# First groups of three weight units, square sums by matmul, and a boundary without GpSimd in a two-layer decoder step

## The reference, cut to what matters

```python
def rms_norm(x, g):
    return x * lax.rsqrt(jnp.mean(x * x, axis=-1, keepdims=True) + EPS) * g

for l in range(2):
    h = rms_norm(x, norm_mix_pre[l])
    mix = mixer_ab(h, ...) if l == 0 else mixer_c(h, ...)      # h @ w_in, mixing, @ w_out
    x = x + rms_norm(mix, norm_mix_post[l])
    h = rms_norm(x, norm_ffn_pre[l])
    a, b = jnp.split(h @ w_up, 2, axis=-1)
    a, new_prev = causal_dwconv(a, prev, conv_w)               # three taps along the tokens
    x = x + rms_norm((jax.nn.gelu(a) * b) @ w_down, norm_ffn_post[l])
```

## Time and profile before

| | us |
|---|---|
| median of 3 runs | 1489.02 (1487.93 to 1490.28) |
| the profiled execution | 1488.02 |
| its span, first to last instruction | 1486.2 |
| TensorE busy | 1394.4 (94% of the span) |
| VectorE busy | 867.9 (58%) |
| ScalarE busy | 557.0 (37%) |
| GpSimd busy | 318.5 (21%) |
| mean granted TensorE clock | 0.966 of 2.4 GHz |

### The profile page before, as it was taken

The page is one execution under the profiler, slowest core; times in us unless marked ns, Lnnn a source line. Parts: engine busy times, 40 slices in busy tenths (PEclk is TensorE's granted clock), DMA queues, the critical chain, the costliest instruction groups (busy, mean ns, idle before and its releaser), DMA issues.

```text
span 1486.2 us, 27553 instructions
## 1 busy us (share of the span) xinstructions
PE 1394.4 (94%) x10588; PEld 1357.5 (91%) x10588; DVE 867.9 (58%) x1319; ACT 557.0 (37%) x1022; POOL 318.5 (21%) x405
## 2 busy tenths in 40 slices
PE   9899997999999999977999999989799999999995
PEld 8887896999999999967899898889699999999995
DVE  6356538665656522268877878864766566563224
ACT  5234334433333322235544444433443333332221
POOL 2123224111111100143222223221511111111002
PEclk9989998999999999989999999989899999999998
DMA  7311131222222322221222212112122222233211
GB/s 262 102 34 53 58 88 37 90 85 87 92 88 85 117 94 82 75 72 57 73 86 86 83 68 78 60 72 87 44 84 87 92 90 85 85 111 110 78 39 60
DMA packets 38526, 123.32 MB, mean 83 GB/s; under 512 B 4104, under 2 KB 9864, under 8 KB 38344
## 3 DMA queue, kind: packets, MB, share of 16 engines
q1 hardware_dynamic: 31888, 110.74, 23.0%
q10 hardware_dynamic: 6408, 11.38, 2.1%
q0 software_dynamic: 176, 0.44, 0.1%
HBM read 113.98 MB, written 8.57 MB: 82 GB/s over the span
## 4 chain that ended last, share of the span: by engine, by line
PE 76%; DVE 15%; issue 4%; ACT 3%; ACTq 1%; DMA 0%; DVEq 0%; POOL 0%; SPq 0%
PE acc L365 67%; DVE w_lo L1036 2%; PE aux L576 2%; DVE x L1237 2%; DVE mix L1232 1%; DVE lev L1334 1%; PE aux L613 1%; PE acc L383 1%; DVE v_s L1489 1%; DVE scratch L1440 1%; DVE h_lo L1044 1%; DVE lev L1328 1%; PE aux L487 1%; DVE c_E L1491 1%; PE aux L467 1%
## 5 line engine op out<-in xcount | busy, mean ns | idle before, releaser
L1036 DVE TENSOR_TENSOR w_lo<-raw,w_hi 128x512 fp32r<-128x512 f32 (+1 forms) x372 | 320.5, 864 | 401.3 <-ACT w_hi L693 400.4
L365 PE MATMUL acc<-h_hi,w_hi 128*128 128x272 f32 x2208 | 477.1, 298 | 35.8 <-DVE h_lo L1044 32.2
L365 PE MATMUL acc<-h_hi,w_lo 128*128 128x272 f32 x2208 | 464.8, 293 | 0.0
L365 PE MATMUL acc<-h_lo,w_hi 128*128 128x272 f32 x2208 | 463.9, 292 | 0.0
L365 PEld LDWEIGHTS acc<-h_hi,w_hi 128*128 128x128 f32 x2208 | 355.4, 193 | 46.8 <-issue 26.5
L693 ACT CAST w_hi<-raw 128x512 fp32r<-128x512 f32 (+1 forms) x372 | 238.4, 643 | 423.4 <-PE acc L365 410.1
L365 PEld LDWEIGHTS acc<-h_lo,w_hi 128*128 128x128 f32 x2208 | 355.9, 193 | 0.0
L365 PEld LDWEIGHTS acc<-h_hi,w_lo 128*128 128x128 f32 x2208 | 353.1, 193 | 0.0
L365 PE MATMUL acc<-g_hi,w_lo 128*128 128x272 f32 x684 | 141.6, 288 | 0.0
L365 PE MATMUL acc<-g_hi,w_hi 128*128 128x272 f32 x684 | 141.4, 288 | 0.0
L365 PE MATMUL acc<-g_lo,w_hi 128*128 128x272 f32 x684 | 141.0, 288 | 0.0
(11 more groups left out here) (244 smaller groups left out, 1640.8 us busy)
## 6 DMA issues: line engine op xcount, KB each, us to landing
raw<-in_w_up SPq DMA_DIRECT2D x88, 512.0 KB, 3.4
raw<-in_w_down SPq DMA_DIRECT2D x32, 704.0 KB, 4.0
raw<-in_w_in_c SPq DMA_DIRECT2D x32, 512.0 KB, 3.5
raw<-in_w_in_ab SPq DMA_DIRECT2D x18, 512.0 KB, 3.8
raw<-in_w_out_ab SPq DMA_DIRECT2D x8, 512.0 KB, 3.5
S<-in_state ACTq DMA_DIRECT2D x8, 512.0 KB, 4.2
o_ss<-Snew ACTq DMA_DIRECT2D x8, 512.0 KB, 2.6
raw<-in_w_out_c SPq DMA_DIRECT2D x8, 512.0 KB, 3.5
```

The costliest lines, as they stand in the source:

```text
L365: mm = pe.matmul(acc[out][:, t, 0:H], w[slot][:, cols], mv[:, kk_, t * H:(t + 1) * H], start=start and k == 0 and q == 0, stop=stop and k ...
L1036: dve.tensor_tensor(w_lo[n % 2][:, to], raw[n % 4][:, cols], w_hi[n % 2][:, to], ALU.subtract).then_inc(lo_ready, 1)
```

## The change

- **Groups of three.** `first_pair` on TensorE becomes `first_group`: units 0, 1 and 2 of in_ab, up0, in_c and up1 are run together, k by k. Unit 1 of a group lies in a third weight slot, unit 2 in the slot that unit 1 had (`slot_of`). Its weights are split ahead of the phase: halves 2, 3 and 4 before `last_out` of the phase before, half 5 after it; in in_ab between the first h tiles (k < 3 instead of k < 2).
- **Four accumulators.** The eight banks are acc[0] to acc[3]; A[0] to A[3] are the banks of acc[2] and acc[3]. The up phases use four in turn (`UP_ACC`), with evacuation waits two units looser; unit 2 of a group uses acc[2].
- **Square sums on TensorE.** For the pre norms the squares go into eight tiles `sq`. TensorE sums them over the tiles: tile j of four onto output partitions 32j to 32j+31, in one call after k = 5 and one within k = 7 (`square_sums`). ScalarE and VectorE copy the two sums to S[2], and two matmuls by ones follow after the first half of unit 3 (`pre_stats`); `norm_root` divides by 32 D.
- **No GpSimd at boundaries.** VectorE scales all eight mix tiles; the order is mix(k), h_lo(k−1), x(k) instead of mix(k), h_lo(k−2), x(k). GpSimd keeps the sums of squares of the post norms only.
- **Early splits.** In the first two pairs of up0 and up1, halves 6 to 9 are split right after the group, 10 and 11 in pair 0; none in pair 1. In in_c halves 6 to 9 come after the group, 10 and 11 in its ticks 6 and 7, which now hold recurrence steps of unit 3 alone.
- **Stores.** SyncE issues the stores of the convolution states, ahead of the x stores; a scratch size for DMAs is set.

```diff
+GROUPS = ("in_ab", "up0", "in_c", "up1")
+UP_ACC = (0, 3, 2, 1)
+def slot_of(n, fixed=True):
+    for name in GROUPS:
+        if fixed and n - UNIT0[name] == 1:
+            return 2
+        if fixed and n - UNIT0[name] == 2:
+            return (n + 1) % 2
+    return n % 2
...
-        acc = [... for i in range(2)]
-        A = [bank(f"aux{i}") for i in range(4)]
+        acc = [... for i in range(4)]
+        A = [acc[2][:, 0, :], acc[2][:, 1, :], acc[3][:, 0, :], acc[3][:, 1, :]]
...
         def halves_at(t, first, up=False):
-            return {0: (), 1: (5, 6), 2: ()}.get(t, (t + 4,)) if first else (t + 4,)
+            if not first:
+                return (t + 4,)
+            return {1: (6, 7, 8, 9), (2 if up else 6): (10,), (3 if up else 7): (11,)}.get(t, ())
...  (TensorE)
+            def first_group(name, norm):
                 for k in range(8):
-                    for u in range(2):
-                        half(m + 2 * u + e, 0, u, h, 4 * e, ...)
-                stats(norm)
+                    d = k // 4
+                    for u in ((0, 1, 2) if k < 7 else (2, 0, 1)):
+                        half(m + 2 * u + d, 0, u, h, 4 * d, ..., ks=[k % 4],
+                             signal={(0, 3): 1, (0, 7): 1, (1, 7): 4}.get((u, k), 0), also=third_done if (u, k) == (2, 7) else None)
+                        if (u, k) == (2, 5):
+                            square_sums(norm, 0)
+                        if (u, k) == (2, 7):
+                            square_sums(norm, 1)
+            def square_sums(norm, d):
+                for j in range(4):
+                    pe.wait_ge(sq_ready, KD * norm + 4 * d + j + 1)
+                    for t in range(2):
+                        mm = pe.matmul(A[2 + t][32 * j:32 * j + 32, 0:H], ones[:, 0:32], sq[:, 4 * d + j, t * H:(t + 1) * H],
+                                       start=d == 0, stop=d == 1)
+            def pre_stats(norm):
+                for t in range(2):
+                    pe.wait_ge(sums_taken, norm + 1 + t)
+                    pe.matmul(A[2 + t][:, 0:H], ones[:], S[2][:, t * H:(t + 1) * H], start=True, stop=True
+                              ).then_inc(stat_done, 1)
...  (ScalarE, split)
+                if unit == [2] and s > 5:
+                    act.wait_ge(half_done, s - 5)
+                if unit == [3]:
+                    act.wait_ge(third_done, [UNIT0[name] < n for name in GROUPS].count(True))
...  (VectorE, first_pair)
+                split(m + 6, 0)
+                dve.wait_ge(sq_summed, norm // 2 + 1)
+                dve.wait_ge(sums_taken, norm + 1)
+                dve.tensor_copy(S[2][:, H:T], A[3][:, 0:H]).then_inc(sums_taken, 1)
...  (VectorE, boundary)
                 for k in range(KD):
-                    if k % 2 == 0:
-                        step.mark(dve.tensor_tensor(mix[:, k, :], mix[:, k, :], S[3][:], ALU.mult))
-                    else:
-                        dve.wait_ge(mix_scaled, KD // 2 * (pre - 1) + 1 + k // 2)
-                    lo(k - 2)
+                    step.mark(dve.tensor_tensor(mix[:, k, :], mix[:, k, :], S[3][:], ALU.mult))
+                    if k == 2 and pre < 4:
+                        split(2 * UNIT0[name] + 5, 0)
+                    lo(k - 1)
```

More of the change, by code:

```diff
@@ L96, with half_cols @@
 HALF = (KFH + 1) // 2 * P
+def half_cols(slot, h):
+    return h * (HALF if slot < 2 else 4 * P)
 class Steps:
@@ L368, in half @@
                     mm.then_inc(half_done, signal)
+                if also is not None:
+                    mm.then_inc(also, 1)
             def keep_warm(n):
                 for _ in range(n):
-                    pe.matmul(A[3][:, 0:P], ones[:], ones[:], start=True, stop=True)
+                    pe.matmul(A[1][:, 0:P], ones[:], ones[:], start=True, stop=True)
             def last_half(m, moving, kt_base):
@@ L404, in stats @@
                     for t in range(2):
-                        if src is S[1] and t == 0 and norm % 2:
-                            pe.wait_ge(sq_cols, (norm + 1) // 2)
-                        else:
-                            pe.wait_ge(ready, count * (norm + 1))
-                        mm = pe.matmul(A[t][:, 0:H], ones[:], src[:, t * H:(t + 1) * H], start=src is S[2],
+                        if src is S[1] and t == 0:
+                            pe.wait_ge(sq_cols, done + 1)
+                        else:
+                            pe.wait_ge(ready, count)
@@ L410, in stats @@
+                        mm = pe.matmul(A[2 + t][:, 0:H], ones[:], src[:, t * H:(t + 1) * H], start=src is S[2],
                                        stop=src is S[1])
@@ L499, in _ @@
             keep_warm(12)
[L500 to L503, removed]
+            first_group("in_ab", 0)
+            for u in range(3, 18):
+                pe.wait_ge(evac, 2 if u < 5 else u - 1)
                 for e in range(2):
@@ L529, in ffn @@
                 norm = 2 + 4 * layer
-                def up(i, units):
-                    for u in units:
-                        pe.wait_ge(evac, TILE0[name] + u - 1 + 4 * i)
-                        for e in range(2):
[L535 to L540, removed]
+                first_group(name, norm)
+                pe.wait_ge(evac, TILE0[name] + 2)
+                for e in range(2):
+                    half(2 * (UNIT0[name] + 3) + e, 0, 1, h, 4 * e, e == 0, e == 1)
+                    if e == 0:
+                        pre_stats(norm)
+                pe.wait_ge(rstd_ready, 2 * (norm + 1))
+                with pe.Fori(1, KF // 2) as i:
+                    for u in range(4):
+                        pe.wait_ge(evac, TILE0[name] + u - 3 + 4 * i)
+                        for e in range(2):
+                            half(2 * (UNIT0[name] + u) + e, 8 * i, UP_ACC[u], h, 4 * e, e == 0, e == 1)
                 name = f"down{layer}"
@@ L903, in down @@
                         for t in range(4):
+                            if last and t == 2 and layer == 0:
+                                group_splits(2 * UNIT0["in_c"])
                             if last and t == 3:
                                 last_out(3 + 4 * layer)
-                            split(2 * UNIT0[name] + 4 * e + t + 4 + s_off, 8 * i if s_off == 0 else 0)
+                                if layer == 0:
+                                    split(2 * UNIT0["in_c"] + 5, 0)
+                            elif not last or t < 2:
+                                split(2 * UNIT0[name] + 4 * e + t + 4 + s_off, 8 * i if s_off == 0 else 0)
                         if not last:
@@ L1275, in up @@
                                 continue
-                            for q in halves_at(t, first and u == 0):
-                                split(2 * UNIT0[name] + 4 * u + q + s_off, 8 * i if s_off == 0 else 0)
+                            for q in halves_at(4 * u + t if first else t, first, True):
+                                split(2 * UNIT0[name] + (0 if first else 4 * u) + q + s_off, 8 * i if s_off == 0 else 0)
                             if t == 1:
@@ L1305, in down @@
                         for t in range(4):
-                            if t == 3 and e == 1 and s_off > 0:
+                            last = e == 1 and s_off > 0
+                            if last and t == 3 and layer == 0:
+                                group_splits(2 * UNIT0["in_c"])
+                            if t == 3 and last:
                                 last_out(2 * UNIT0[name] + 8 + s_off, 2 + 2 * layer)
```

224 lines of the change are left out of this document (118 added, 106 removed).

## The result

| | before | after |
|---|---|---|
| median | 1489.24 us (1487.83 to 1490.46, 7 runs) | 1496.28 us (1493.67 to 1498.26, 7 runs) |
| the profiled execution | 1488.02 | 1496.82 |
| its span | 1486.2 | 1495.0 |
| mean granted TensorE clock | 0.966 | 0.963 |

The ratio is 1.0045, interval 1.0034 to 1.0057: slower by 7.0 us. The forecast was 1496.6, and the likeliest of its cases came. (The ratios given here are not the quotients of the two medians; these can differ from them by up to 0.0007.)

The account below looks back on a forecast made before the run. The prediction took TensorE's matmul time (76% of the span) plus its waits to bound the kernel. Its terms +6.8 + 0.9 + 0.0 + 0.9 − 1.0 = +7.6 us gave 1495.6 profiled, 1496.6 against the median, range 1492 to 1500.

Parts of the forecast that it names:

- the likeliest of its cases: Whole kernel: slower, about 1496.6 us against the median, chance 0.55.
- start: Start of the kernel: +6.8 us from unit 2's weight wait, clock, square sums less old statistics, and readout; bounds +4.5 and +8.5.
- half 12 split, behind the second root: In up0, half 12 (unit 6) is split only after the gated pairs and a table load, 19.0 us behind the second root.
- wait at unit 6: In up0, TensorE finishes units 3, 4, 5 and waits 5.4 us for half 12.
- start of unit 6 against before, from the first x: In up0, unit 6 begins 1.4 us earlier than before (−1.4).
- up0, up1: Each up phase loses net 0.9 us, bounds −1.4 and +1.6; up1's timeline repeats before's.
- in_c: At in_c, root 3.0 us later but kt_s at 692.6: gain 0.2, taken as 0 (−0.5 to +1.0).
- The main step: At the up0 boundary, the last h_lo ends 5 us earlier, but TensorE then waits 5.4 us for half 12.
- the lead is kept: Rival, chance 0.18: TensorE keeps 5.8 us at each of three boundaries, giving 1477.4 us; with half the lead, 1486.
- The one on serial square sums: Rival, chance 0.10: square sums run one by one, +5.6 us at four groups, giving 1519; half so, 1508.
- No change: Rival, chance 0.17: unit 2's weight wait costs 4.5 us in all, clock stays high in waits; +0.7, giving 1489.7.
- The clock behind the wait: In up0, after the wait for half 12, 3.3 to 5.7 us at half rate cost 1.7 to 2.9 us, taken as 2.3.

Follow-up runs that it names:

- e2: Changed kernel with halves 12 to 19 split ahead, in pairs 1 to 3 of both up phases: 1488.62 us, ratio 1.0004 to the kernel before.
- e9: Changed kernel with halves 12 to 19 split ahead, vv's readout earlier and the start's unit 2 deferred, no unread matmuls: 1483.51 us, ratio 0.9968 to the kernel before.
- e5: Changed kernel with unit 2 of the first projection fitted in from k = 4 on, its splits behind tile 4: 1491.12 us, ratio 1.0021 to the kernel before.
- e3: Changed kernel with vv's readout at in_c moved from step 5 to step 1, behind the rescale of qn: 1496.35 us, ratio 1.0052 to the kernel before.
- e6: Changed kernel with 44 unread matmuls in in_c's wait before the transposes of kd: 1495.97 us, ratio 1.0057 to the kernel before.
- e7: Changed kernel with the edits of e2, e3, e4, e5 and e6 together: 1479.62 us, ratio 0.9940 to the kernel before.
- e8: Kernel before with 28 unread matmuls at the head of the first pairs of up0, in_c and up1: 1489.38 us, ratio 1.0004 to the kernel before.
- e4: Changed kernel with 16 unread matmuls at the head of the groups of three in up0, in_c and up1: 1492.16 us, ratio 1.0023 to the kernel before.

## Why the prediction was right, step by step

| step | predicted | measured |
|---|---|---|
| start | +6.8 | +6.6 |
| wait for unit 2 | 3.1 | 2.81 (2.8 to 3.5 in six traces) |
| half clock of the start | 2.8, before 2.0 | 2.8, before 1.7 (from the distances of the matmuls) |
| two square sums | 2.4 | 2.14 (30.00 − 28.93, twice), 2.5 with their edges |
| readout wait at unit 3 | 1.1 | 0.82 |
| last h_lo behind the root | 19.7 | 19.6 |
| group's end behind the root | 26.4 | 26.5 |
| second root behind the group's end | 6.5 | 6.4 |
| half 12 split, behind the second root | 19.0 | 19.4 |
| wait at unit 6 | 5.4 | 5.78 |
| start of unit 6 against before, from the first x | −1.4 | −1.1 (up0), −1.3 (up1), five traces |
| up0, up1 | +0.9 each | +0.6, +0.1 |
| in_c: root against before; vv's transposes behind it | +3.0; 12.9 | +2.5; 14.4 |
| in_c | 0.0 | +0.8 |
| end | −1.0 | −1.1 |
| sum | +7.6 | +7.0 |

The main step, that five microseconds won at the boundary are spent waiting for half 12, is shown twice: by the chain of the trace after, and by e2 and e9, where splitting ahead gave 1.8 to 4.6 us back in a phase. The rival "the lead is kept" is what e2 makes of the kernel. The one on serial square sums fell with 1.07 us for 16 passes. "No change" asked for a cheaper start; e5 shows what that takes.

Two terms were off. in_c was put at nothing because kd and kt_s would come early enough. The added wait on vv's readout was not read: it held the transposes for the 0.9 to 1.0 us that e3 gives back. The clock of the stretch was not counted either: e6 gives back 0.6 at the same transposes. With both gone, in e7, they start 12.9 us behind the root, where the prediction had them.

The other term is up0 and up1, +0.9 each. It has a slip in its sum and a price that was too high. The terms written out for half 12 (9.3, 7.7, 1.28, 0.6, 0.65) add up to 19.5, not 19.0, so the wait should have been put at 5.9 and the start of unit 6 at −0.9; the trace has 19.4, 5.78 and −1.1. The clock behind the wait was priced at 2.3; in the trace after it cost 1.9 (nine pairs of matmuls from 288.42 to 292.56, 4.14 us instead of 9 × 0.25). −1.1 with +1.9 makes +0.8, near the +0.6 of the table. up1 lost less than up0: its unit 6 starts 0.2 earlier and its half clock behind the wait is some 0.3 us shorter, which makes 0.3 of the 0.5; the rest is within the scatter of the traces.

That the total came within 0.6 us of the forecast is in part luck: in_c was 0.8 too low and the two up phases together 1.1 too high.

## What to carry to other kernels

A lead won on one engine lasts only to the next item that another engine's hand-written list releases late: look for that item (here half 12 behind a table load) and move it before widening anything. Weights that land during a group should be used last in it: deferring them in TensorE's order gave 3.6 us where moving the load up gave nothing that could be told. Clock that is lost where another engine sets the pace cost nothing (e8) or 0.7 us (e6) here; where TensorE set it, unread matmuls in the wait paid (e4, 3.3 us).

## What the runs showed of the hardware

- 16 passes of 272 columns onto 32 output partitions, in four column groups, took 1.07 us to the start of the next matmul; full-width passes at 0.25 would take 4.0, and four abreast 1.0. The pair ahead and the pair behind are 0.1 us longer each than the 0.25 of the others, so the call costs 1.27 with its edges. The Trainium skill (TensorEngine Tiling (Array Packing), Key Properties) says that a change of tiling mode drains TensorE; in this trace both changes together cost less than 0.3 us, and that is a bound and not the price of a drain: behind the full-width statistics in the same kernel (266.52 us), where no mode changes, the next pair is 0.2 longer as well.
- The stretch in_c b, out_c took 360.6 to 363.7 us in twelve traces, the two kernels of the old order among them at 361.4 and 363.7; no edit of an experiment reaches into it. Stretches of half clock of 3.4 to 6.8 us fall there in different places from one trace to the next. A difference of 2 us in a long stretch between two single traces is no finding: the first reading of in_c here, 2.8 us, was 0.8.
- Unread matmuls in the wait kept the granted clock at 1.00 (2.4 GHz) through a boundary (e4_warm, 225 to 265 us; 0.91 in after). In the kernel before they raised the mean clock from 0.966 to 0.978, and its time did not move.
